# Hybrid encoder layer on one core: the inverse softmax sums take a path through VectorE and DRAM, and three steps of the schedule move

## The reference, cut to what matters

```python
h = rmsnorm(x);  z = h @ w_in                      # 1536 tokens: sequences of 1024 and 512
# group A, multi-head latent attention, 4 heads:
s = (q_nope @ k_nope.T + q_rope @ k_rope.T) * MLA_SCALE
p = softmax(s);  o = p @ v                         # bidirectional, each sequence by itself
# group B: pooling mixer; group C: gated linear attention, two directions,
o_gla = rmsnorm(o_fwd + o_bwd)                     # chunks of 64 tokens
mixed = concat(o_mla * silu(g), o_pool * silu(g), o_gla * silu(g))
y = rmsnorm(x + mixed @ w_out)
```

## Time and profile before

| what | value |
|---|---|
| three runs | 745.91, 747.58, 748.26 us; median 747.58 |
| profiled execution, its own time | 750.29 us |
| its span from first to last instruction | 748.5 us |
| busy: TensorE, VectorE, ScalarE, POOL | 96%, 55%, 42%, 38% of the span |
| granted TensorE clock, mean | 0.987 of full speed |

### The profile page before, as it was taken

How to read it: one execution, slowest core, us unless ns; L and a number is a source line. 1 busy time by engine, 2 the same in 40 slices (tenths; PEclk the granted TensorE clock), 3 DMA queues, 4 the chain that set the end, 5 groups by cost and what they waited for, 6 DMA issues and landing times.

```text
span 748.5 us, 14234 instructions
## 1 busy us (share of the span) xinstructions
PE 721.3 (96%) x5784; PEld 606.4 (81%) x5784; DVE 408.9 (55%) x718; ACT 311.9 (42%) x520; POOL 287.6 (38%) x290
## 2 busy tenths in 40 slices
PE   8999999999999999999999789889989999999996
PEld 6998878878888888888888588788788988888885
DVE  5855877376575543026175757758656654333232
ACT  6554444334423432233223545555554654232321
POOL 3223226366556512122400255553555854322320
PEclk9999999999999999999999889999999999999999
DMA  7613021001122233230235886786886035564441
GB/s 255 183 26 89 28 97 57 30 31 40 63 72 87 73 114 107 92 88 26 63 144 180 249 240 207 230 225 184 264 233 194 1 109 180 176 196 158 139 151 56
DMA packets 65389, 96.14 MB, mean 128 GB/s; under 512 B 6161, under 2 KB 43537, under 8 KB 65330
## 3 DMA queue, kind: packets, MB, share of 16 engines
q1 hardware_dynamic: 53856, 65.34, 30.3%
q10 hardware_dynamic: 11474, 29.96, 10.6%
HBM read 59.30 MB, written 35.00 MB: 126 GB/s over the span
## 4 chain that ended last, share of the span: by engine, by line
PE 76%; DVE 8%; DMA 7%; ACT 4%; POOL 2%; issue 2%; SPq 0%; ACTq 0%; DVEq 0%; POOLq 0%
PE psum L78 20%; PE psum L80 19%; PE psum L79 19%; PE psum L1535 4%; DMA spread_scratch<-a_spread_second 3%; DVE a_top L2082 2%; PE psum L1374 2%; DMA a_turned_lo_third<-spread_scratch 2%; ACT a_weights L1982 2%; POOL a_turned_lo_third L1895 2%; PE psum L1254 1%; DVE g_state L1062 1%; DVE a_weights L2055 1%; DMA a_turned_lo<-spread_scratch 1%; PE psum L1404 1%
## 5 line engine op out<-in xcount | busy, mean ns | idle before, releaser
L78 PE MATMUL psum<-h_hi,z_w_hi 128*128 128x512 f32 x376 | 152.4, 405 | 0.0
L80 PE MATMUL psum<-h_hi,z_w_lo 128*128 128x512 f32 x376 | 146.8, 390 | 0.0
L79 PE MATMUL psum<-h_lo,z_w_hi 128*128 128x512 f32 x376 | 146.6, 390 | 0.0
L78 PEld LDWEIGHTS psum<-h_hi,z_w_hi 128*128 128x128 f32 x376 | 70.6, 188 | 15.9 <-issue 0.7
L80 PEld LDWEIGHTS psum<-h_hi,z_w_lo 128*128 128x128 f32 x376 | 70.6, 188 | 15.4
L79 PEld LDWEIGHTS psum<-h_lo,z_w_hi 128*128 128x128 f32 x376 | 70.7, 188 | 14.0 <-issue 0.7
L1982 ACT ACTIVATE a_weights<-psum,a_bias,mla_q_scale 128x1024 f32<-128x1024 f32 (+1 forms) x48 | 51.0, 1062 | 64.9 <-DVE a_bias L2085 64.9
L805 POOL TENSOR_TENSOR z_w_lo<-z_w_raw,z_w_hi 128x1024 fp32r<-128x1024 f32 x17 | 41.0, 2411 | 94.5 <-ACT z_w_hi L501 92.4
L78 PE MATMUL psum<-o_w_hi,o_m_hi 128*128 128x512 f32 x184 | 72.6, 394 | 0.0
L80 PE MATMUL psum<-o_w_hi,o_m_lo 128*128 128x512 f32 x184 | 72.3, 393 | 0.0
L79 PE MATMUL psum<-o_w_lo,o_m_hi 128*128 128x512 f32 x184 | 72.2, 392 | 0.0
(11 more groups left out here) (281 smaller groups left out, 1656.5 us busy)
## 6 DMA issues: line engine op xcount, KB each, us to landing
z_w_raw<-in_w_z_dram SPq DMA_DIRECT2D x17, 512.0 KB, 3.6
n_x_in<-in_x_dram SPq DMA_DIRECT2D x12, 512.0 KB, 4.3
gates_scratch<-z_gate ACTq DMA_DIRECT2D x24, 256.0 KB, 2.1
spread_scratch<-a_weights ACTq DMA_DIRECT2D x12, 512.0 KB, 5.0
spread_scratch<-a_spread_second ACTq DMA_DIRECT2D x12, 512.0 KB, 6.6
a_turned_lo<-spread_scratch SPq DMA_DIRECT2D x24, 256.0 KB, 5.2
o_x_in<-in_x_dram SPq DMA_DIRECT2D x12, 512.0 KB, 3.6
out_dram<-o_y ACTq DMA_DIRECT2D x11, 512.0 KB, 3.2
```

The lines of the kernel that those rows point to most:

```text
L78: nc.tensor.matmul(out, a_hi, b_hi, start=first, stop=False)
L79: nc.tensor.matmul(out, a_hi, b_lo, start=False, stop=False)
L80: return nc.tensor.matmul(out, a_lo, b_hi, start=False, stop=last)
```

## The change

Four parts.

- **Shares by DRAM.** TensorE's 48 transposes of shares and VectorE's 24 copies of them go. `take_share` of an odd step now also transposes 32x32 blocks of the pair's share columns on VectorE (`share_rows`), which leaves the shares in rows, 32 queries in each of four partition groups. SP stores these with four DMAs of two rows of 128 bytes each (`store_shares`) and loads the 1 KB back, broadcast to 128 partitions, into the pair's place in `mixed` (`load_shares`). `gather` is one multiplication in place. For pairs 0 to 17 both stand in SP's loop around the loads of the pair; for pairs 18 to 23 they stand behind the w_out loads.
- **High parts in one step.** `take_high` for both tiles of a pair at odd steps, behind latent_hi.
- **Values nine steps behind.** `values(p)` at 2p + 9 for most pairs up to 14 (pair 1 at 12), output and gather with it; the last pairs as before but for pair 16 (40 for 39).
- **Points merged.** In the front, `compare(t)`, `output(t - 1)` and `turn_rows(t - 3)` stand at one point 3t.

```diff
-                if t >= 2:
-                    act.wait_ge(o_mm, t - 1)
+                if t >= 1:
+                    act.wait_ge(o_mm, t)
                 nc.scalar.activation(attn[:, t % 2, :, :], psum[:, 2:2 + HEADS, 0:CHUNK], ACT.Copy).then_inc(top_copied, 1)
...
                 if at == 0:
+                    if 1 <= t <= TILES:
+                        take_rows(t - 1)
                     if t < TILES:
                         copy_top(t)
+                    if t % 4 == 2 and 6 <= t < TILES + 3:
+                        take_outputs(t // 4 - 1)
                     if t % 2 == 1 and t + 1 < TILES:
                         end_exponentials(t // 2 + 1)
                 if at == 2:
-                    if t < TILES:
-                        take_rows(t)
-                    if t % 4 == 1 and 1 < t < TILES + 2:
-                        take_outputs(t // 4 - 1)
                     if t % 2 == 1 and t // 2 + 2 < UNITS:
                         exponentials(t // 2 + 2)
...
-                if t:
-                    scale_rows(t - 1)
-                sum_rows(t)
+                if t >= 2:
+                    scale_rows(t - 2)
+                if t >= 1:
+                    sum_rows(t - 1)
 
             def split_w_q():
...
-                    pe.wait_ge(o_taken, t)
+                    if t >= 2:
+                        pe.wait_ge(o_taken, t - 1)
                 pe.wait_ge(q_ready, GROUPS * u + GROUPS)
                 pe.wait_ge(k_ready, GROUPS * u + GROUPS)
...
-                if p >= 0 and p % 3 == 0 and p // 3 < TILES:
-                    compare(p // 3)
-                if p >= 2 and p % 3 == 2 and p // 3 < TILES + 2:
-                    if p // 3 >= 2:
-                        turn_rows(p // 3 - 2)
-                    if p // 3 < TILES:
-                        output(p // 3)
+                t = p // 3
+                if p >= 0 and p % 3 == 0 and t < TILES + 3:
+                    if t < TILES:
+                        compare(t)
+                    if 1 <= t <= TILES:
+                        output(t - 1)
+                    if t >= 3:
+                        turn_rows(t - 3)
 
             def project_early(j, steps):
...
 SPREAD_PAIRS = LAST_HEAD // 2
 TURN_LAG = 2
-VALUES_AT = tuple(2 * p + 8 for p in range(SPREAD_PAIRS - 2)) + (39, 41, 42, 44, 45, 47, 49, 51)
-LATE_OUTPUTS = SPREAD_PAIRS - 2
+VALUES_AT = (9, 12) + tuple(2 * p + 9 for p in range(2, SPREAD_PAIRS - 3)) + (38, 40, 41, 42, 44, 45, 47, 49, 51)
+LATE_OUTPUTS = SPREAD_PAIRS - 5
 OUTPUT_AT = tuple(m + (2 if p < LATE_OUTPUTS else 1) for p, m in enumerate(VALUES_AT))
 GATHER_AT = tuple(m + 1 for m in OUTPUT_AT)
...
+        rest, q_rope = keep.rest, keep.q_rope
         top = rest("a_top", [P, STEPS])
         bias = rest("a_bias", [P, STEPS])
         total = rest("a_total", [P, STEPS])
-        share = rest("a_share", [P, STEPS])
+        share = rest("a_share", [P, STEPS + SPREAD])
+        share_rows = rest("a_share_rows", [P, 2, SPREAD])
         assert rest.at <= keep.w_out_hi_at
 
...
+            def store_shares(p):
+                if p:
+                    sp.wait_ge(share_passed, 80 * p)
+                sp.wait_ge(share_ready, 3 * p + 4)
+                for a in range(4):
+                    sp.dma_start(share_dram[p][:, a * SPREAD:(a + 1) * SPREAD], share_rows[a * SPREAD:a * SPREAD + 2, p % 2, :])\
+                      .then_inc(share_passed, 16)
+
+            def load_shares(p):
+                sp.wait_ge(share_passed, 80 * p + 64)
+                sp.dma_start(mixed_of(p), share_dram[p].rearrange("n t -> (n t)").partition_broadcast(P))\
+                  .then_inc(share_passed, 16)
+
             for b in range(TB):
                 sp.wait_ge(front.rope_stored[b], 64)
                 load_rope(0, b)
             for p in range(SPREAD_PAIRS):
                 count = keys_of(2 * p)
+                store_shares(p)
                 for n in range(2):
                     sp.wait_ge(spread_stored[n], 16 * p + 16)
...
+                load_shares(p)
...
+            for p in range(SPREAD_PAIRS, PAIRS):
+                store_shares(p)
+                load_shares(p)
 
         @block.gpsimd
...
-                    pool.wait_ge(gathered, 3 * TILES + 2)
+                    pool.wait_ge(gathered, SPREAD_PAIRS + 1)
...
-                    take_high(m - 5)
                 for p in pair_at(m, VALUES_AT):
                     act.wait_ge(values_done, p + 1)
                     nc.scalar.activation(latent_hi[:, p % 2, :], psum[:, 6 + p % 2, :PAIR], ACT.Copy)\
                       .then_inc(latent_hi_ready, 1)
+                if m % 2 and 5 <= m < LAST_HEAD + 5:
+                    take_high(m - 5)
+                    take_high(m - 4)
...
             def gather(p):
-                h, t = p // (2 * TB), (p % (2 * TB)) * PAIR
                 dve.wait_ge(output_done, p + 1)
-                nc.vector.tensor_copy(share_row[:, p % 2, :], psum[:, 6 + p % 2, PAIR:]).then_inc(gathered, 1)
-                dve.wait_ge(gathered, 2 * p + 1)
-                nc.vector.tensor_tensor(keep.mixed[:, h, t:t + PAIR], psum[:, 6 + p % 2, :PAIR],
-                                        share_row[:, p % 2, :], ALU.mult).then_inc(gathered, 1)
+                dve.wait_ge(share_passed, 80 * p + 80)
+                nc.vector.tensor_tensor(mixed_of(p), psum[:, 6 + p % 2, :PAIR], mixed_of(p), ALU.mult).then_inc(gathered, 1)
 
             def take_share(m):
                 nc.vector.reciprocal(share[:, m:m + 1], total[:, m:m + 1]).then_inc(share_ready, 1)
+                if m % 2:
+                    p = m // 2
+                    dve.wait_ge(share_ready, 3 * p + 3)
+                    if p >= 2:
+                        dve.wait_ge(share_passed, 80 * (p - 1))
+                    nc.vector.transpose(share_rows[:, p % 2, :], share[:, 2 * p:2 * p + SPREAD]).then_inc(share_ready, 1)
 
...
+                if LAST_HEAD < m <= STEPS:
+                    dve.wait_ge(exp_done, m)
+                if 1 <= m <= STEPS:
                     take_share(m - 1)
                 for h, b in projected_at(m):
...
                     tile = m - TURN_LAG
-                    dve.wait_ge(exp_done, tile + 1)
-                    take_share(tile)
...
-                    pe.wait_ge(gathered, 2 * p - 2)
+                    pe.wait_ge(gathered, p - 1)
...
-                pe.wait_ge(share_ready, 2 * p + 2)
                 pe.wait_ge(latent_lo_ready, p + 1)
-                for n in range(2):
-                    nc.tensor.transpose(psum[:, 6 + p % 2, PAIR + n * P:PAIR + (n + 1) * P],
-                                        share[:, 2 * p + n:2 * p + n + 1].broadcast_to([P, P]), ident[:, :])
...
+        share_dram = scratch("share_scratch", (PAIRS, 2, P), F32)
...
```

More of the change, by code:

```diff
@@ L1217, in split_rope @@
                                             ALU.subtract).then_inc(rope_lo, 1)
+            scale_rows(TILES - 2)
+            sum_rows(TILES - 1)
             scale_rows(TILES - 1)
@@ L1647, in __init__ @@
         self.mix_first = rest("o_mix_first", [P, 4, P])
-        self.share_row = rest("a_share_row", [P, 2, PAIR])
         self.rest = rest
@@ L1771, in portion, with phase_mla_attend @@
     return slice((m % 2) * keys_of(m), (m % 2 + 1) * keys_of(m))
-def phase_mla_attend(nc, cx, block, front, rope_dram, gates_dram, mix_dram, spread_dram, w_out_dram, w_out_loaded, gate_loaded, mix_loaded, psum,
-                     ident, keep):
+def phase_mla_attend(nc, cx, block, front, rope_dram, gates_dram, mix_dram, spread_dram, share_dram, w_out_dram, w_out_loaded, gate_loaded, mix_loaded,
+                     psum, ident, keep):
     with ExitStack() as mem:
@@ L1794, in phase_mla_attend @@
         spread = [weights[:, 2, :], spread_second[:, :]]
-        rest, q_rope, share_row = keep.rest, keep.q_rope, keep.share_row
+        rest, q_rope = keep.rest, keep.q_rope
         top = rest("a_top", [P, STEPS])
@@ L1807, in phase_mla_attend @@
         share_ready = sem("a_share_ready")
+        share_passed = sem("a_share_passed")
         transposed = sem("a_transposed")
@@ L1837, in weights_slot, with mixed_of @@
             return m % 2 if m < LAST_HEAD else (m - LAST_HEAD) % SLOTS
+        def mixed_of(p):
+            return keep.mixed[:, p // (2 * TB), (p % (2 * TB)) * PAIR:(p % (2 * TB) + 1) * PAIR]
         def by_key(parts, p):
@@ L2022, in _ @@
                     project(h, b)
-                if 5 <= m < LAST_HEAD + 5:
-                    take_high(m - 5)
                 for p in pair_at(m, VALUES_AT):
@@ L2073, in _ @@
             dve.wait_ge(front.rope_stored[0], 64)
+            nc.vector.memset(share[:, :], 0.0).then_inc(share_ready, 1)
+            dve.wait_ge(share_ready, 1)
             for m in range(GATHER_AT[-1] + 1):
@@ L2302, in weight_gates @@
                 nc.gpsimd.tensor_tensor(mix[s][:, :, :], mix[s][:, :, :], gate[s][:, 4:8, :], ALU.mult).then_inc(gated, 1)
-            pool.wait_ge(attend.gathered, 2 * PAIRS)
```

(3 more changed lines are left out.)

## The result

| | before | after |
|---|---|---|
| median of the runs | 747.92 us (745.91 to 748.28, 4 runs) | 761.75 us (760.59 to 762.47, 4 runs) |
| ratio of after to before | | 1.0181, 95% interval 1.0156 to 1.0205 |
| profiled execution, its own time | 750.29 us | 762.47 us |
| its span | 748.5 us | 760.7 us |

The change costs 13.8 us in the median and 12.2 in the span. The forecast was 753.5 us, 5.9 more, with a range of 737 to 764: the direction was right and so was SP's part of the mechanism (its serial rounds), but the size was less than half of what was measured, and a wait of VectorE that the prediction did not have is in it.

What follows compares the result with a forecast made beforehand. TensorE, busy 721.3 of 748.5 us, bounds the kernel, so gains come from its stream or gaps; SP's serial rounds cost. The tail's +5.9, with the attention phase's +2.0 hidden inside, on a median of 747.58 gives 753.5 us, range 737 to 764.

Steps and rivals of the forecast that it cites:

- The points merged: Front: twelve pairs of TensorE visits to the linear attention become one each, 0.15 us per tile, -1.8 us.
- The transposes: Attention phase: 24 pairs' share transposes leave TensorE, 5.0 us, counting only where TensorE sets the pace.
- High parts and values: Attention phase: low parts freed one step earlier, values one step later, each taking part of the gaps; nothing counted.
- SP's round: SP's queue: four stores, burst of loads, share load landing in series; 9.6 us for 1024 keys, 7.3 for 512.
- near 149: Expected sign in SP's queue: the 17 spacings between bursts take near 149 us, before 140.
- Where this meets TensorE: Pair 15 lands at 554.0, so values(15) starts at 559.8 instead of 555.95: +3.9 us.
- VectorE: VectorE loses 24 copies of 0.41 us and gets 24 transposes of 0.12 to 0.41; nothing counted.
- The tail: Behind w_out: six serial share rounds of 5.8 us delay the second tile's gate to 617.7, +5.9 us at the end.
- the 2.0: End of the attention phase: values(15) 3.9 later, less 1.9 for nine pairs' transposes, +2.0 us, hidden inside the final delay.
- the queue's 5.9: SP's queue behind w_out: the second tile's gate is issued 6.5 us later, TensorE had 0.6 to spare, +5.9 us.
- Dear issues: Rival: SP's small stores cost 0.56 us each, 0.44 more per round over 23 rounds, +10.1, 763.6 us; chance 0.10.
- The queue does not hold: Rival: share loads land soon after issue, rounds take 5.8 us, TensorE sets the pace, -14.9, 732.7 us; chance 0.31.

Runs made afterwards that it cites:

- experiment 4: The changed kernel, serial wait kept, with eight instead of two buffers for the turned shares, so VectorE's wait goes: 758.59 us, ratio 1.0143.
- experiment 5: The kernel without the serial wait, plus an SP wait for the previous pair's four loads, not its share load, before each pair's share stores: 751.73 us, ratio 1.0038.
- experiment 1: The changed kernel without SP's serial wait; share stores and loads count on separate semaphores for even and odd pairs: 743.93 us, ratio 0.9945.
- experiment 10: The kernel before with only the shares by DRAM as in the change (serial wait, two buffers): 761.91 us, ratio 1.0189.
- experiment 8: The kernel before with merged points, both high parts in one step and values nine steps behind, shares still on TensorE: 744.53 us, ratio 0.9957.
- experiments 7: The kernel before with the merged points alone: 744.96 us, ratio 0.9965.
- experiment 3: The changed kernel, serial wait kept, with share stores and loads of pairs 18 to 20 placed between the w_out loads: 756.59 us, ratio 1.0110.
- experiment 2: The changed kernel without the serial wait, and each share load issued one round later, ahead of the next pair's stores: 743.01 us, ratio 0.9940.
- experiment 6: The changed kernel, serial wait kept, with each pair's share load issued ahead of its four loads instead of behind: 767.96 us, ratio 1.0270.

## Why the prediction was right or wrong

Taken by the ratios, from 1.0181 down: VectorE's wait for a free buffer 2.8 us (experiment 4), the landing of the share load behind its burst 7.8 (5), the landing of the burst itself 7.0 (5 against 1), and what is left is 4.1 us faster than before, for which the points (2.6) are the one part that showed an effect by itself. Each of the three terms is uncertain by 2.5 to 3.6 us; the traces, not the ratios, say where they are.

- **The points merged: -1.8 forecast, -2.6 measured (-0.9 to -4.4).** Not told apart. In the changed kernel it doesn't show, where SP's rounds set the pace (experiment 10).
- **The transposes: up to 5.0, "only where TensorE sets the pace".** No gain shows. With SP free, the shares on TensorE gave 744.53 (experiment 8) and by DRAM 743.93 (experiment 1): 0.9 us by the ratios, not told apart.
- **High parts and values: nothing.** None shows with the shares on TensorE (experiments 7 and 8).
- **SP's round.** The mechanism held line by line. The stores were cheaper than taken: mostly 1.1 to 1.6 us for four (0.25 each) and 1.46 from the first store to the burst in the mean, not 1.8. The burst was mis-sized for 1024 keys: 8.1 in the mean (experiment 5), where I had 7.6 between ends of 7.5 and 8.8; pair 15's, from 549.87 to the high part that waited for it at 557.36, took 7.5. The share load behind it is 0.1 to 0.3, against 0.2; behind 512 keys it is 1.0, not 0.4, made good by a burst of 4.9 instead of 5.1 and the cheaper stores. So the round of 1024 keys is **10.0 us, not 9.6**, and that of 512 is 7.3, as forecast. From burst to burst there are twelve rounds of 1024 keys and five of 512, so its own terms make 151.7, not the "near 149" that it gives for the 17 spacings; measured are 156.5. Over the rounds to pair 15 this put its loads at 557.36 instead of 554.0.
- **Where this meets TensorE: +3.9 at values(15).** They started at 564.67, 8.7 later than before; at pair 17 the kernel was still 7.2 late, where the prediction had 2.0 for the end of the phase. Of the 4.8 that values(15) was later than forecast, 3.4 are the load. For the rest TensorE did not wait for this pair at all: POOL had its low parts ready at 563.23, and TensorE came straight from the scores. The path was another one: in the whole phase it waited 1.3 us for POOL's low parts, the one path that was priced, and 29 for ScalarE and VectorE, in whose streams the waits for the tiles' loads (47.2) and for the share loads (25.0) stand.
- **VectorE: "I count nothing". This is the step that failed.** I priced the transpose (0.21 us measured, within the range) and not the wait in front of it. `share_passed` at 80(p - 1) ties VectorE's step of pair p to the share load of pair p - 2, and in the last head this load stands behind w_out. I followed the new wait on SP to everything queued behind it, and did not do the same for the new wait on VectorE. Measured: 7.15 us of VectorE at pair 18's low parts, 5.2 of the kernel at that place; taking the wait away gave 2.8 (experiment 4) to 5.3 us (experiment 3) by the ratios. It is not all that was missing. Without it the kernel is still 10.7 us above the one before by the ratio and 8.3 by the span, where 5.9 was forecast: the rest is in the round and in the path to TensorE, above.
- **The tail.** w_out's first load was issued at 569.81 (567.9 forecast), and its last issue ended at 586.39 (584.4): right to 2 us. The rounds behind it, forecast at 5.8 us each, took 6.9, 5.0 and 5.2 where only their landings set them (in the first the stores landed in 3.10 us, in the other two in 0.84; the loads took 2.9 to 3.2; forecast were 2.2 for each), and 8.2 and 5.9 where SP waited for VectorE's shares. But I had them pay at the end, through the second tile's gate, with TensorE's delay hidden inside. They paid at their beginning, at pair 18, through VectorE; the gate, issued at 623.66 (617.7 forecast), had to wait 3.2 us for TensorE's last values, so the queue was no longer what held it, and no wait of TensorE for the second token tile shows. So the forecast that the 2.0 would vanish in the queue's 5.9 did not come true: the kernel was 7.2 late before w_out's shares and 12.4 behind them. These two are not independent either. The chain goes through SP's queue to VectorE, so a TensorE that was less late would have waited longer for the same share load; this is argued from the chain, no run shows it.
- **The rivals.** "Dear issues" has the nearest time, 763.6, by luck: stores took 0.25 us each, not 0.56. "The queue does not hold" is refuted by SP's 72.0 us, and its price was wrong as well: with SP freed the time is 743 to 744, not 732.7, since 15.6 us (experiment 2) to 18.2 (experiment 1) of TensorE's waits remain and change only their releaser.

The rival "The queue does not hold" rested on half a rule. In the round of pair 15 SP was released by the share load at 557.96, 0.6 us after the burst had let ScalarE go. It was so in every round of the 17 in which ScalarE waited for the burst: SP was released 0.2 to 1.5 us later, never before it. The same section of the Trainium skill ("DMA: Bandwidth & Descriptors", on queues, rings and completion order) goes on to say that the semaphore's increment, unlike the data, is written only after every earlier write of that DMA engine. By that half of the rule a wait on the share load is a wait for the burst ahead of it, as far as both use the same DMA engines. The trace of the changed kernel agrees with it; before, the first `load_rope` landed 0.9 us ahead of its burst.

## What to carry to other kernels

When a change makes a queue wait for its own last transfer, look where the same semaphore count is waited for elsewhere: here one counter for stores and loads tied SP to the full landing of a pair and VectorE to the load of two pairs back. Separate semaphores per kind and parity cost nothing and took all of the loss away. A small transfer issued behind a burst was as late as the burst here (0.2 to 1.5 us later), so its waiter waits for the burst too. And waits that vanish in front of one engine come back under another name when the pace is set by a chain through several: price a removed wait by what is late next, not by its length. Of the change, the merged points are worth keeping; shares by DRAM without the serial wait (743.0 to 743.9) are not told apart from the points alone (745.0).

## What the runs showed of the hardware

- Four 256-byte stores cost SP 1.11 us to issue in a row (0.25 each), less than a load of a burst (0.45). Their landing is what can cost, and it depends on what else is under way. Counted from the end of the last issue it took 0.84 us with SP's queue otherwise empty (594.47 to 595.31), 3.10 with the last w_out load just ahead (issued at 586.06, 512 KB, landed 3.9 later), and 4.18 beside a tile's store of ScalarE's queue (experiment 6).
- A wait that stops TensorE costs more than its length. After the 3.16 us wait that ended at 594.70 its products of 256 columns follow each other in 0.21 us until about 600.3, and then in 0.12. The granted clock was 0.50 from 594.70 to 600.40 (the lower level, 1.2 GHz) and 1.00 from there to 610. At the upper level these 5.7 us of work would have taken about half, an estimate from the two spacings of products: 2.4 to 2.8 us on top of the wait. Over the whole span the granted clock was 0.987 before and 0.980 after. First the busy time and the clock of a wider stretch (its 0.84 is the mean over 20 us), then two pairs of products from TensorE's timeline, all of after:

```profile
580.00:600.00 20.00, 16.29 (x93) 0.84 0.40 120
```

```profile
599.22 0.41 PE L78 MATMUL psum<-a_turned_hi_second,mla_tokens_hi 128*128 128x256 f32 x1
599.43 0.41 PE L79 MATMUL psum<-a_turned_lo_second,mla_tokens_hi 128*128 128x256 f32 x1
...
600.83 0.28 PE L78 MATMUL psum<-a_turned_hi_second,mla_tokens_hi 128*128 128x256 f32 x1
600.95 0.28 PE L79 MATMUL psum<-a_turned_lo_second,mla_tokens_hi 128*128 128x256 f32 x1
```
